# A two-block transformer on one core: compression with stationary token blocks, the first expert slot gathered by products, and later recurrence gates

## The reference

```
def compress(k, pos, w1, b1, w2, b2):          # windows of 32 tokens, 16 apart: 31 of them per group
    win = (windows(k) + pos).reshape(..., 32 * 64)
    return gelu(win @ w1 + b1) @ w2 + b2        # w1 2048 x 256, w2 256 x 64; once for keys, once for values
def hybrid_mixer(h, ...):                       # once in each of the two layers
    q, kc, vc, ks, vs, kw, vw, gates, u, bg, cg = split(h @ w_in)
    ... compressed, selected and window attention, gated; short convolution; @ w_o
def moe_swiglu(h, w_router, wg, wu, wd):        # layer 1; 8 experts, 2 for each token, width 1408
    gate = softmax(top_k(h @ w_router, 2))
    out = sum(gate_e * (silu(h @ wg_e) * (h @ wu_e)) @ wd_e)
# second block: RMSNorm, projections X (recurrence input), Z and others; per 128 channels of X:
#   a convolution over 4 tokens; two 128 x 128 gate products (R, IX) and sigmoids; a = exp(c * softplus * R);
#   h_t = a_t h_(t-1) + sqrt(1 - a_t^2) * IX * x_t; then times silu(Z), dilated attention, w_o, RMSNorm
```

## Time and profile before

| | |
|---|---|
| median of 3 runs | 2484.21 us (2478.0 to 2484.8) |
| the profiled execution: its own time | 2482.89 us |
| its span in the trace | 2481.1 us |
| mean granted clock of PE | 0.97 |
| PE busy | 2323.6 us, 94% |
| DVE, ACT, POOL busy | 1445.4, 1162.0, 544.6 us |
| DMA moved | 436.00 MB, 176 GB/s |

### The profile page before, as it was taken

The page is one execution under the profiler, slowest core; times in us unless marked ns, Lnnn a source line. Parts: engine busy times, 40 slices in busy tenths (PEclk is TensorE's granted clock), DMA queues, the critical chain, the costliest instruction groups (busy, mean ns, idle before and its releaser), DMA issues.

```text
span 2481.1 us, 29748 instructions
## 1 busy us (share of the span) xinstructions
PE 2323.6 (94%) x11044; PEld 1833.3 (74%) x11044; DVE 1445.4 (58%) x1987; ACT 1162.0 (47%) x1469; POOL 544.6 (22%) x230
## 2 busy tenths in 40 slices
PE   6999999999999999689999999999957899999998
PEld 5866777788778667377887778777745588777786
DVE  5277674611352675777887888888855580245342
ACT  3244342222332444376766777677734552334333
POOL 3111324434422112200000000000012344323242
PEclk9999999999989999889999999999978999999999
DMA  7211238823342111399999999999952233322231
GB/s 218 53 43 43 72 100 249 249 78 99 104 121 72 51 43 52 122 340 351 358 362 360 356 358 364 366 366 366 346 187 64 76 88 100 94 68 69 61 98 63
DMA packets 381092, 436.00 MB, mean 176 GB/s; under 512 B 12944, under 2 KB 287808, under 8 KB 380992
## 3 DMA queue, kind: packets, MB, share of 16 engines
q1 hardware_dynamic: 359268, 402.31, 48.5%
q10 hardware_dynamic: 19420, 23.95, 3.2%
q0 software_dynamic: 2304, 8.39, 0.8%
HBM read 410.50 MB, written 22.02 MB: 174 GB/s over the span
## 4 chain that ended last, share of the span: by engine, by line
PE 56%; issue 32%; DVE 6%; DMA 3%; ACT 2%; POOL 1%; ACTq 0%; DVEq 0%; SPq 0%; POOLq 0%
PE bank L810 20%; PE bank L814 10%; PE bank L1052 5%; PE bank L1314 5%; DMA mod_raw<-in_w_mod_dram 2%; PE bank L940 2%; PE bank L1027 2%; PE bank L1088 2%; PE bank L1069 2%; PE bank L837 2%; PE bank L841 1%; PE bank L829 1%; DVE mod_sum L2056 1%; ACT head L1444 1%; PE bank L1353 1%
## 5 line engine op out<-in xcount | busy, mean ns | idle before, releaser
L751 POOL TENSOR_TENSOR rest<-raw,head 128x1024 fp32r<-128x1024 f32 (+1 forms) x210 | 524.3, 2501 | 1091.5 <-ACT head L1444 1091.4
L2323 DVE TENSOR_TENSOR rest_m<-raw_m,head_m 128x2048 fp32r<-128x2048 f32 (+2 forms) x270 | 567.5, 2112 | 132.9 <-ACT head_m L1505 132.1
L1505 ACT ACTIVATE head_m<-raw_m 128x2048 fp32r<-128x2048 f32 (+2 forms) x270 | 477.1, 1774 | 203.8 <-DMA raw_m<-in_moe_wu_dram 71.8
L1444 ACT ACTIVATE head<-raw 128x1024 fp32r<-128x1024 f32 (+1 forms) x210 | 225.2, 1076 | 250.4 <-PE bank L814 197.2
L810 PE MATMUL bank<-HH,head 128*128 128x512 f32 x760 | 307.2, 404 | 15.7 <-ACT head L1444 15.7
L810 PE MATMUL bank<-HL,head 128*128 128x512 f32 x760 | 301.8, 397 | 0.0
L1184 PE MATMUL bank<-head_m,XH 128*128 128x512 f32 (+1 forms) x720 | 280.8, 390 | 8.3 <-DVE rest_m L2323 6.2
L1184 PE MATMUL bank<-rest_m,XH 128*128 128x512 f32 (+1 forms) x720 | 271.7, 377 | 0.0
L1184 PE MATMUL bank<-head_m,XL 128*128 128x512 f32 (+1 forms) x720 | 271.5, 377 | 0.0
L814 PE MATMUL bank<-HH,rest 128*128 128x512 f32 x760 | 192.6, 395 | 0.0
L810 PEld LDWEIGHTS bank<-HH,head 128*128 128x128 f32 x760 | 144.5, 190 | 58.7 <-ACT head L1444 17.7
(11 more groups left out here) (406 smaller groups left out, 3843.8 us busy)
## 6 DMA issues: line engine op xcount, KB each, us to landing
raw_m<-in_moe_wd_dram SPq DMA_DIRECT2D x75, 1024.0 KB, 8.4
raw_m<-in_moe_wg_dram SPq DMA_DIRECT2D x60, 1024.0 KB, 6.8
raw_m<-in_moe_wu_dram SPq DMA_DIRECT2D x60, 1024.0 KB, 8.0
raw<-in_w_in_dram SPq DMA_DIRECT2D x110, 512.0 KB, 4.0
raw_m<-in_moe_wg_dram SPq DMA_DIRECT2D x30, 768.0 KB, 6.1
raw_m<-in_moe_wu_dram SPq DMA_DIRECT2D x30, 768.0 KB, 5.1
raw<-in_w_o_dram SPq DMA_DIRECT2D x24, 512.0 KB, 3.9
mod_raw<-in_w_mod_dram ACTq DMA_DIRECT2D x12, 1024.0 KB, 6.6
```

The source lines that it names most:

```text
L751: pool.tensor_tensor(rest[slot][:, 0:kt, :], raw[slot][:, 0:kt, :], head[slot][:, 0:kt, :], ALU.subtract).then_inc(weights_split, 1)
L1444: act.activation(head[slot][:, 0:kt, :], raw[slot][:, 0:kt, :], ACT.Copy).then_inc(head_done, 1)
L1505: act.activation(head_m[slot][:, 0:width], raw_m[slot][:, 0:width], ACT.Copy).then_inc(gran_head, 1)
L2323: dve.tensor_tensor(rest_m[slot][:, 0:width], raw_m[slot][:, 0:width], head_m[slot][:, 0:width], ALU.subtract).then_inc(gran_split, 1)
```

## The change

Four things are changed.

1. Compression. `A2` becomes stationary (65 strided columns: 62 windows and one position column) and `W1` moving (256 contiguous columns): 32 products into two banks, with windows along the partitions. DVE copies the 65 by 256 result to `hid`; after the gates tile PE multiplies it, in four pieces of 128 columns, with a small table `pick` (identity, with ones in row 64), which turns it back to hidden channels along the partitions and adds the position row. ACT applies gelu with the bias, now behind the sigmoid of the gates.
2. `together` runs two tiles side by side, and with `third` the three products per chunk of a third tile follow two chunks behind. ACT's `keys` makes the head of tile n0+3 ahead of the first copies and the head of the following one no longer in `keys(1)`.
3. Entry of the experts. DVE forms from the ranks a one-hot table of expert 0's rows (`hot`, 4 instructions, with `iota` from an extra product), and PE makes slot 0's transposed rows as 32 fp32 products of `H_tok` with `hot`, without the way through DRAM. The owners are worked out later on DVE (behind the first `turned`), ACT and DVE take the transposed rows ahead of the last weight pieces, SP waits for the owners and issues granules 4 to 6 ahead of its wait for the scattering, and only slot 1 is read back there. ACT's scaling of `H_tok` moves behind the first four granules.
4. Recurrence. PE's order is: tile X3+k, gates k, for all k, so that gates 5, 6 and 7 follow Z0, Z1 and Z2. ACT takes X two tiles ahead: `conv_in(0)`, `conv_in(1)`, and in the loop `conv_in(k+2)` ahead of the sigmoids of k.

```diff
@@ compression, PE
                 for kv in range(2):
+                    for tp in range(CMP_PAIRS):
+                        last = pe.matmul(bank[3 + kv][0:65, 0:256],
+                                         A2[:, kv, :, :].rearrange("p g n -> p (g n)")[:, tp:tp + 8 * 64 + 1:8],
+                                         W1[:, kv, tp, :], start=(tp == 0), stop=(tp == CMP_PAIRS - 1))
+                    last.then_inc(hid_done, 1)
+                tile(n0 + M_GATES, HH, HL)
+                for kv in range(2):
+                    pe.wait_ge(hid_taken, 2 * l + kv + 1)
                     for m in range(2):
-                        b = bank[3 + 2 * kv + m]
-                        for tp in range(CMP_PAIRS):
-                            last = pe.matmul(b[:, 0:3 * NCMP].rearrange("p (g n) -> p g n", g=3),
-                                             W1[:, kv, tp, m * P:(m + 1) * P],
-                                             A2[:, kv, :, tp:tp + 8 * (NCMP - 1) + 1:8],
-                                             start=(tp == 0), stop=(tp == CMP_PAIRS - 1))
-                        last.then_inc(hid_done, 1)
-                tiles(n0 + M_GATES, 2, HH, HL)
+                        pe.matmul(bank[5 + kv][:, m * 64:m * 64 + 2 * NCMP], hid[:, kv, m * P:(m + 1) * P],
+                                  pick[0:65, :], start=True, stop=True).then_inc(hid_done, 1)
+                tile(n0 + M_GATES + 1, HH, HL)
@@ together, PE: the third tile
+            def together(n0, hi, lo, ready_hi, ready_lo, order=range(KT), third=True):
...
+                def behind(j):
+                    n, k = n0 + 2, order[j]
+                    slot = n % RING
...
+                    for w, x in ((head, hi), (head, lo), (rest, hi)):
+                        last = pe.matmul(bank[slot][:, :], w[slot][:, k, :], x[:, k, :],
+                                         start=(j == 0 and w is head and x is hi), stop=(j == KT - 1 and w is rest))
...
+                    if third and j >= 2:
+                        behind(j - 2)
                 low(KT - 1)
+                if third:
+                    behind(KT - 2)
+                    behind(KT - 1)
@@ keys, ACT
-                    if kind > 0:
+                    if kind > 1:
                         heads_ahead(n, 1)
                     act.wait_ge(tile_done, n + 1)
+                    if kind == 0:
+                        make_head(n0 + 3)
@@ experts_in, SP
-                sp.wait_ge(x_scattered, 16 * 2 * ST)
-                slot_rows(0)
-                slot_rows(1)
                 sp.wait_ge(owner_ready, 1)
                 for d in range(OVER):
                     owner.append(bass.ds(sp.value_load(exi[0:1, d:d + 1], min_val=0, max_val=EXPERTS - 1), 1))
+                for g in range(GRAN, GRAN + 3):
+                    granule(g, owner[0])
+                sp.wait_ge(x_scattered, 16 * 2 * ST)
+                slot_rows(1)
@@ experts, PE
-                wait_rows(0, 0, 0, 0)
+                pe.wait_ge(ht_ready, 2 * ST)
+                pe.wait_ge(hot_ready, ST)
                 for a_ in range(2):
-                    turn(a_, a_, lambda c: xs[0][:, (4 * a_ + c) * P:(4 * a_ + c + 1) * P], 4)
+                    for c in range(4):
+                        k = 4 * a_ + c
+                        for t in range(ST):
+                            last = pe.matmul(bank[4 + a_][:, c * P:(c + 1) * P], H_tok[:, t, k * P:(k + 1) * P],
+                                             hot[:, t, :], start=(t == 0), stop=(t == ST - 1))
+                    last.then_inc(turn_done, 1)
@@ router, DVE
+                step(dve.tensor_copy(rank0[:, :], ranks[:, :, 0]))
+                for t in range(ST):
+                    dve.tensor_scalar(hot[:, t, :], iota[:, :], rank0[:, t:t + 1], sel[:, t, 0:1], ALU.is_equal, ALU.mult) \
+                       .then_inc(hot_ready, 1)
@@ block 2, PE
-            for k in range(3, KT):
-                tile(B2_X + k, HH, HL)
-                lru_gates(k - 3)
-            lru_gates(KT - 3)
-            lru_gates(KT - 2)
-            tile(B2_Z, HH, HL)
-            lru_gates(KT - 1)
-            for n in range(B2_Z + 1, B2_RNN):
+            for k in range(KT):
+                tile(B2_X + 3 + k, HH, HL)
+                lru_gates(k)
+            for n in range(B2_Z + 3, B2_RNN):
@@ block 2, ACT
             conv_in(0)
+            conv_in(1)
             for k in range(KT):
-                if k + 1 < KT:
-                    conv_in(k + 1)
-                if k >= KT - 2:
+                if k + 2 < KT:
+                    conv_in(k + 2)
+                else:
                     make_head(B2_Z + k - KT + 4)
```

More of the change, by code:

```diff
@@ L816, in tile @@
                 last.then_inc(tile_done, 1)
-            def together(n0, hi, lo, ready_hi, ready_lo, order=range(KT), count=3):
-                pe.wait_ge(head_done, n0 + count)
-                for n in range(n0, n0 + count):
+            def together(n0, hi, lo, ready_hi, ready_lo, order=range(KT), third=True):
+                pe.wait_ge(head_done, n0 + 2)
+                for n in range(n0, n0 + 2):
                     if n >= RING:
@@ L930, in mixer @@
                     pe.wait_ge(hl_ready, first)
-                together(n0, HH, HL, *normed(KT * 2 * l), count=first)
+                together(n0, HH, HL, *normed(KT * 2 * l), third=(l == 1))
                 tiles(n0 + first, M_GATES - first, HH, HL)
@@ L988, in mixer @@
                 L, n1 = 2 * l + 1, n0 + N_PROJ
-                together(n1, MH, ML, head_in, rest_in, order=[4, 5, 6, 0, 1, 2, 7, 3], count=2)
+                together(n1, MH, ML, head_in, rest_in, order=[4, 5, 6, 0, 1, 2, 7, 3], third=False)
                 tile(n1 + 2, MH, ML)
@@ L1131, in router @@
             def router():
+                pe.matmul(bank[7][:, 2 * P:3 * P], ones[:, :], cst[:, K_TRI:K_TRI + P], start=True, stop=True) \
+                  .then_inc(lg_done, 1)
                 pe.wait_ge(rw_landed, 16)
@@ L1654, in _ @@
                 heads_ahead(n0 + M_Q, 5)
-                for kv in range(2):
-                    for m in range(2):
-                        j = 2 * kv + m
-                        act.wait_ge(bsum_ready, 4 * l + j + 1)
-                        act.activation(HG[:, kv, m, :], bank[3 + j][:, 0:2 * NCMP], ACT.Gelu_apprx_tanh,
-                                       bias=bsum[:, j:j + 1]).then_inc(gelu_ready, 1)
                 n = n0 + M_GATES
@@ L1664, in _ @@
                 take(act.activation(GT[:, :], bank[n % RING][0:3 * HEADS, :], ACT.Sigmoid), n)
+                for kv in range(2):
+                    act.wait_ge(hid_done, 6 * l + 2 * kv + 4)
+                    for m in range(2):
+                        act.activation(HG[:, kv, m, :], bank[5 + kv][:, m * 64:m * 64 + 2 * NCMP], ACT.Gelu_apprx_tanh,
+                                       bias=col("cmp_b1", 4 * l + 2 * kv + m)).then_inc(gelu_ready, 1)
                 keys(2)
@@ L2305, in router, with owners @@
                 dve.tensor_copy(idx[:, :], posk[:, :]).then_inc(lg_ready, 1)
+            def owners():
+                steps = cst[:, K_STEP:K_STEP + EXPERTS]
                 step(dve.tensor_tensor(over[:, :], over[:, :], first[:, :], ALU.add))
@@ L2380, in iteration @@
                             product(3 * s + 3, (hf + 1) % 2, g0 + 11, GU0)
-                for g in range(GRAN):
-                    split_rest(g, g, 2048)
+                split_rest(0, 0, 2048)
                 for a_ in range(2):
@@ L2386, in experts @@
                     turned(a_, a_, XL[0][:, rows, :], XH[0][:, rows, :], 4)
+                    if a_ == 0:
+                        owners()
+                        split_rest(1, 1, 2048)
+                for g in (2, 3):
+                    split_rest(g, g, 2048)
                 dve.wait_ge(gate_raised, 1)
```

64 lines of the change are left out of this document (40 added, 24 removed).

## The result

| | before | changed |
|---|---|---|
| median of the runs | 2484.19 us (2475.03 to 2484.85, 7 runs) | 2459.03 us (2446.17 to 2461.21, 7 runs) |
| ratio | | 0.9902 (0.9879 to 0.9925) |
| profiled execution: time, span | 2482.89, 2481.1 us | 2459.73, 2457.9 us |

What follows compares the result with a forecast made beforehand. PE, busy 94% of the span, was taken as the bound, except the experts, bound by DMA. 2482.9 - 11.0 - 1.25 - 3.3 - 8 - 7.5 = 2451.9, with 1.3 for the median 2453; range 2442 to 2468, forecast's own 2446 to 2459.

Steps and rivals of the forecast that it cites:

- rival C: Experts' entry: early granules only push the scattering back, so the entry gives 0 to 2 us; time 2460, chance 0.12.
- Compression: Compression in both layers: 21.6 us becomes 14.9 plus 1.2 us, gaining 5.5 us a layer, 11.0 in both.
- the strided block is hidden: Compression: loading the strided stationary block, 0.14 us a record, hides behind products of 0.233 us.
- Feed-forward head: Feed-forward stage: the 1.26 us wait for a head made by ACT goes, -1.25 us.
- Second mixer: Second layer's mixer: idle 3.22 us and half clock go, less a new wait; net -3.3 us (-1.5 to -5).
- the new wait: Second layer's mixer: a tile waits for the bank that DVE's third Q copy frees, 1.7 us.
- Experts: Entry of the experts: weight stream starts earlier, granules 4 to 6 leaving at about 1048.6; -8 us (-5 to -12).
- Recurrence: Block 2 gates: period 7.46 instead of 9.30 us, then PE stands at Z3's bank; -7.5 us (5 to 9).
- Rival D: Recurrence: ACT's chain does not hold Z3, or the stall is made up; 15 us instead of 7.5, 2445, chance 0.08.
- Rival F: Removed waits return a tile later at banks DVE and ACT free; only compression and experts remain; 2465, chance 0.08.
- B: Compression: the strided stationary block sets the pace, no gain from 0.33 us a record on; 2464, chance 0.14.
- E: Compression: strided stationary block eats all other gains, slower from 0.475 us a record on; 2490 at 0.52, chance 0.03.

Runs made afterwards that it cites:

- late-granule kernel: The changed kernel, but SP issues granules 4 to 6 only when the scattering is complete: 2458.3 us, ratio 0.9895.

## Why the prediction was right, and where its terms were off

The direction, and that no single part carries the change, came as forecast. The time, 2459, lies 6 us above the 2453 of the sum, in the stated range and at the upper end of the forecast's own (2446 to 2459); rival C's 2460 is nearer to it, and which of the two holds is read from the traces and not from the time. That the sum came so near is in part luck: in the two profiles compression and recurrence gave 5.3 us more than their terms, feed-forward, mixer and experts 9.2 us less, and some 4 us were lost where no term stood. Term by term:

- **Compression, -11.0 forecast, -14.2 measured.** The step that the strided block is hidden was right, and now rests on a row (0.12 under 0.213). Mis-sized was the column price. The two rows that I took it from don't give the same 0.91 ns, as I wrote: the 128 columns of the earlier trace rows are 0.79 ns a column and record (0.101/128), the 512 columns of the earlier trace rows 0.91 (0.465/512). The new records with 256 columns have 0.83 (0.213/256), between the two, so 13.6 us and not 14.9; and the eight turning records took 0.81 and not 1.2 us. The 0.068 us that stood for a contiguous block was misread: the 16 records of the earlier trace rows start in pairs 0.006 us apart, one pair every 0.109 us, so it was the pace of two blocks side by side. The strided price worked out from it, 0.14, came near the 0.12 by luck.
- **Feed-forward head, -1.25 forecast, +0.8 in the pair and about -0.9 at equal clock.** The wait of the earlier trace rows did go, and the stretch from the stage's first product to the first single tile fell from 20.9 to 19.1 us. But the whole stage takes 390.8 to 394.0 us with the new form and 391.9 and 392.5 with the old one. In the pair shown here PE was at half clock at the end of the stage from 701.7 instead of 708.5: the granted clock of the last 69 us was 0.91, and of the last 66 us before the change 0.94. What a closed wait earned there, the clock took back in this trace. With half of the time at half clock taken off, the stage is 385.7 and 386.1 us in the two traces with the old form and 384.7 to 385.3 in the twelve with the new one: about 0.9 of the 1.25 us came. The clock itself takes 5.8 to 9.3 us of the stage, which the sum had no term for.
- **Second mixer, -3.3 forecast, -0.4 measured.** The failing term is the new wait: I left 1.7 us for it. It was 0.79 us for the key copy, 2.42 for the query bank, together as long as the 3.22 us that went, and then a second switch to half clock, which I had counted as gained and not as a price of the new wait. With the time lost to half clock taken off, the stretch is 36.7 us in the old form and 37.0 to 37.1 in the new one, so even the 0.4 us is the clock's. The mechanism named (the Q take behind the A2 copies) is right: with that one take moved, 4.0 to 4.2 us came.
- **Experts, -8 forecast, -3.7 measured at granule 17.** Two steps failed. Granule 4 was to leave 12.3 us behind the ranks and left 15.1: the products took 9.0 us instead of 7.5, because 3.4 us of them were at half clock (five other traces at full clock have 7.4 and granule 4 at 13.7), and the seven loads with their wait 5.8 instead of 4.2. But an earlier granule 4 alone would not have given more, since granule 17 is no earlier in those five. The second step: the room in the DMA engines was counted over 20 us at a share of 0.65, while the granules came only for the last part of it; from 1046 they shared 1.04 with the scattering, which then landed 4.7 us later behind its last issue. The prediction made that rival C and gave it 0 to 2 us: its mechanism is shown by the 5.1 us of the late-granule kernel and by the 1.9 us of the five traces with earlier granules; the size of the whole entry, 3.7, lies between C's and the 8 of the sum. From router to last product the medians of the traces are 798.2 us new and 800.4 old, so at the end of the stage at most some 2 us can be seen, inside the spread.
- **Recurrence, -7.5 forecast, 7 to 8 measured**, and 1.6 more from the third X tile, of which I had counted 0.9. Period (7.46 forecast, 7.3), the wait at Z3's bank (5 to 8 forecast, 7.22), and what holds it (ACT's place for the take) are as written. Rival D, that Z3 would not have to wait, falls; that the stall is worth 5 us more shows when the take is moved.
- **What no term held:** the start of the kernel and the attention of layer 0 differ by 4 us between the two profiles, 2.9 of them time at half clock. All traces together put these two stretches anywhere in 60.7 to 63.5 and 229.5 to 232.4 us, whatever the kernel.

Rival F (what is removed comes back a tile later at banks that DVE and ACT free) holds in the second mixer and for 7 us of the recurrence, as the sum had it, and not beyond. B, D and E fall, and C holds for the mechanism.

## What to carry to other kernels

When a wait for one resource of a ring is closed, go on in the timeline to the next one who must free something in the same ring, and move that take in the same change: the query take and the Z takes, a few lines each, gave 4 and 5 us. Turning a product around (the short strided operand stationary, the long contiguous one moving) paid here, and should as long as the load of the block stays under the time of the moving columns. And for a transfer sent ahead of one that is still under way, count the idle share at that moment, not the mean share of the stretch: here, granules that left 1.4 us earlier went with a granule 17 that came 1.3 us later.

## What the runs showed of the hardware

- A stride of 8 fp32 elements at least doubled both the reading of moving columns (0.169 us for 93, against 0.073 to 0.085 by the two contiguous prices) and the loading of 65 stationary columns (0.12 against 0.059 us a record, beside 64 moving columns).
- The weight stream of the experts, at a DMA share of 0.99 to 1.00, took from 700.8 to 713.5 us for the same 252 granules in 13 traces. A change of some 4 us could not be judged here by the run times of 10 and 13 executions.
- Behind waits of 1.84 us (the first of the earlier trace rows), 2.30 us (Z3 with the early takes), 2.42 us (query bank), 3.22 us, 6.26 us and 7.22 us (Z3) PE worked at half clock for 2.8 to 4.0 us, which costs 1.4 to 2.0 us on top of the wait, whatever its length. But not every wait has this price: the four of 1.72 us lie in a stretch (1903.1 to 1950.9) whose granted clock is 1.00 throughout, and nor has the one of 0.78 us ahead of the query tiles.
